# The seams between the stages of two chained transformer blocks, taken by token tile

## What is computed

```python
x = x + 0.5 * gate0 * swiglu(modulate(x, w0, shift0, scale0), w13[0], w2[0])     # FFN 0, 2816 hidden
x = x + gate1 * hybrid_mixer(modulate(x, w1, shift1, scale1), ...)               # attention and convolution
x = x + 0.5 * gate2 * swiglu(modulate(x, w2, shift2, scale2), w13[1], w2[1])     # FFN 1
h = rmsnorm(x, norm_mix_g)                                                       # second block
x = x + (gate_a * y_a(h) + gate_b * y_b(h)) @ w_out
x = x + square(relu(rmsnorm(x, norm_mlp_g) @ w_ff1)) @ w_ff2
x = x + sigmoid(rmsnorm(x, norm_ple_g) @ w_ple_gate) * (p @ w_ple)
return rmsnorm(x, final_norm_g)

def modulate(x, w, shift, scale): return rms_norm(x, w) * (1 + scale) + shift
def rmsnorm(x, g): return x * rsqrt(mean(x * x, -1) + 1e-6) * g
```

## Time and profile before

| | us |
|---|---|
| median of 3 runs | 1082.72 |
| lowest, highest | 1081.56, 1084.91 |
| the profiled execution: own time | 1081.31 |
| its span | 1079.4 |
| TensorE busy in the span | 1020.7 |
| VectorE (DVE) busy | 696.8 |
| ScalarE (ACT) busy | 501.0 |

### The profile page before, as it was taken

The page is one execution under the profiler, slowest core; times in us unless marked ns, Lnnn a source line. Parts: engine busy times, 40 slices in busy tenths (PEclk is TensorE's granted clock), DMA queues, the critical chain, the costliest instruction groups (busy, mean ns, idle before and its releaser), DMA issues.

```text
span 1079.4 us, 12967 instructions
## 1 busy us (share of the span) xinstructions
PE 1020.7 (95%) x4788; PEld 839.2 (78%) x4788; DVE 696.8 (65%) x1040; ACT 501.0 (46%) x554; POOL 36.7 (3%) x70
## 2 busy tenths in 40 slices
PE   7999999899989889999999999899999999999996
PEld 5877888688777767888888787777787778888874
DVE  6968777878868667654445895354556565445557
ACT  5553334444664435433344555543453444444452
POOL 0001111001001000000000000000000000000000
PEclk9999999989999999999999999998999999999999
DMA  9967998647637335875455545233334455544531
GB/s 382 414 235 273 329 307 314 236 163 277 269 126 264 117 117 183 317 270 182 186 194 194 224 176 195 78 117 116 128 117 156 179 208 189 195 174 176 195 117 39
DMA packets 37038, 219.41 MB, mean 203 GB/s; under 512 B 4192, under 2 KB 4960, under 8 KB 16006
## 3 DMA queue, kind: packets, MB, share of 16 engines
q1 hardware_dynamic: 26604, 179.70, 44.9%
q0 software_dynamic: 9104, 35.66, 9.4%
q10 hardware_dynamic: 1290, 3.51, 0.9%
HBM read 217.77 MB, written 4.22 MB: 206 GB/s over the span
## 4 chain that ended last, share of the span: by engine, by line
PE 77%; DVE 13%; ACT 5%; DMA 2%; issue 1%; ACTq 0%; DVEq 0%; POOLq 0%; SPq 0%
PE YP L402 11%; PE YP L404 11%; PE YP L403 11%; PE GP L402 10%; PE GP L404 10%; PE GP L403 10%; DVE wlo L1494 4%; ACT whi L1015 2%; PE TP L404 2%; PE TP L403 2%; PE TP L402 2%; DVE arena L1635 1%; DMA raw<-in_stream 1%; DMA ada<-in_ada_t 1%; DVE ada L1626 1%
## 5 line engine op out<-in xcount | busy, mean ns | idle before, releaser
L1494 DVE TENSOR_TENSOR wlo<-raw,whi 128x2048 fp32r<-128x2048 f32 x160 | 365.5, 2290 | 198.2 <-ACT whi L1015 197.9
L1015 ACT ACTIVATE whi<-raw 128x2048 fp32r<-128x2048 f32 x160 | 306.0, 1918 | 281.0 <-PE YP L404 144.4
L402 PE MATMUL GP<-whi,hT 128*128 128x512 f32 x512 | 203.0, 396 | 6.2 <-DVE hT L1584 2.3
L404 PE MATMUL GP<-whi,hT 128*128 128x512 f32 x512 | 199.9, 390 | 0.0
L403 PE MATMUL GP<-wlo,hT 128*128 128x512 f32 x512 | 199.6, 390 | 0.0
L402 PE MATMUL YP<-whi,hT 128*128 128x512 f32 (+2 forms) x320 | 130.2, 407 | 7.0 <-DVE hT L1575 2.5
L402 PE MATMUL YP<-whi,bT 128*128 128x512 f32 x334 | 131.4, 393 | 0.3 <-DVE bT L1681 0.3
L404 PE MATMUL YP<-whi,bT 128*128 128x512 f32 x334 | 130.2, 390 | 0.0
L403 PE MATMUL YP<-wlo,bT 128*128 128x512 f32 x334 | 130.0, 389 | 0.0
L403 PE MATMUL YP<-wlo,hT 128*128 128x512 f32 (+2 forms) x320 | 124.5, 389 | 0.0
L404 PE MATMUL YP<-whi,hT 128*128 128x512 f32 (+2 forms) x320 | 124.3, 389 | 0.0
(11 more groups left out here) (314 smaller groups left out, 1031.8 us busy)
## 6 DMA issues: line engine op xcount, KB each, us to landing
raw<-in_stream SPq DMA_DIRECT2D x161, 1024.0 KB, 4.8
ada<-in_ada_t POOLq DMA_DIRECT2D x48, 512.0 KB, 5.4
arena<-in_ada_t SPq DMA_DIRECT2D x8, 1024.0 KB, 10.7
arena<-in_ada_t POOLq DMA_DIRECT2D x8, 512.0 KB, 6.1
bias_scratch<-bias_row POOLq DMA_DIRECT2D x1, 3072.0 KB, 15.2
ada<-bias_scratch POOLq DMA_DIRECT2D x8, 384.0 KB, 3.9
arena<-in_b_gate ACTq DMA_DIRECT2D x2, 1024.0 KB, 6.5
x<-in_x SPq DMA_DIRECT2D x2, 512.0 KB, 4.0
```

Of the source, the lines that this page charges most:

```text
L402: nc.tensor.matmul(out_ap, xT[0][:, k, tok], hi, start=start, stop=False)
L404: return nc.tensor.matmul(out_ap, xT[1][:, k, tok], hi, start=False, stop=stop)
L1015: nc.scalar.activation(whi[:, slot, :], raw[:, slot, :], ACT.Copy).then_inc(w_hi, 1)
L1494: nc.vector.tensor_tensor(wlo[:, slot, :], raw[:, slot, :], whi[:, slot, :].bitcast(F32), ALU.subtract)\
```

## The change

All five seams go by token tile. The fourth quarter of the residual no longer stands before tile 0's squares and factor. Squares are taken in halves of 512 columns with the factor 1/32 squared in them; the factor has eight operations instead of nine and comes out scaled by RS_SCALE (undone in modA, in the gain row, and by a ninth operation in seams 3 to 5). In seams 1 and 2 ACT scales the left half of a tile and DVE the right half (in seam 2, tile 0, DVE both). The eight transposes of one tile (`turn_tile`) are one step; ACT's shift goes over 128 columns and is followed, for chunks 2 to 7 of tile 0 and all of tile 1, by ACT's own rounding; DVE subtracts. TensorE takes tile 0 through all eight chunks of the two units, and then tile 1 (`project_first`); tile 1's transposes are put in before its first chunk in seams 1 and 2, and before chunk 6 or 4 of tile 0 in seam 3 or 4 and 5. Tile 0's transposes move into the stage before: in seams 3 and 5 ahead of its last quarter of rows, in seam 2 ahead of the last two chunks, in seam 4 ahead of the last four. The bias rows move out of FFN 0 into seam 1. The hand-written orders of ACT and DVE mix the pieces of the residual, of both tiles and of the units' `hi` and `lo`. Not shown below are merged semaphores (`dve_step` for several others, `b_gate`, `bias_in`, `last_loaded`), renamed tiles, and the removed helpers.

```diff
+        ACT_HI = (range(2, KD), range(KD))
...
+            def turn_tile(phase, t):
+                for k in range(KD):
+                    if k % 4 == 0:
+                        if phase < 3:
+                            pe.wait_ge(sig(f"x_{('left', 'right')[k // 4]}{t}"), phase + (t == k // 4))
+                        else:
+                            pe.wait_ge(sig(f"x_part{t}"), summed(phase, k // 4))
+                    if t and k % 2 == 0:
+                        pe.wait_ge(sig("h0"), ready(phase, 0, k + 1))
+                    last = nc.tensor.transpose(x_bank(phase, k)[:, tok(t)],
+                                               (xn if phase < 3 else x)[:, t, k * P:(k + 1) * P], ident[:, :])
+                    if k % 2:
+                        last.then_inc(sig(f"turned{t}"), 1)
+            def project_first(phase, u, outs, insert, width=N):
 
                 for t in range(T):
-                    if phase < 3:
-                        pe.wait_ge(sig(f"x_scaled{t}"), phase + 1)
-                    else:
-                        pe.wait_ge(sig("x_summed"), T * (phase - 1) + t + 1)
                     for k in range(KD):
-                        last = nc.tensor.transpose(x_bank(phase, k)[:, t * P:(t + 1) * P],
-                                                   (xn if phase < 3 else x)[:, t, k * P:(k + 1) * P], ident[:, :])
-                        if t == T - 1 and k % 2:
-                            last.then_inc(sig("x_turned"), 1)
+                        if (t, k) == insert:
+                            turn_tile(phase, 1)
+                        if t == 0 and k % 4 == 0:
+                            pe.wait_ge(w_lo, u + k // 4 + 1)
+                        pe.wait_ge(sig(f"h{t}"), ready(phase, t, k))
+                        last = passes(outs[t][:, 0:width], (hT_hi, hT_lo), k, t, (u + k // 4) % SLOTS, k % 4 * N, width,
+                                      k == 0, k == KD - 1)
+                        if t == T - 1 and k % 4 == 3:
+                            last.then_inc(w_used, 1)
...
-            def last_rows(units, xT):
+            def last_rows(units, xT, phase=None):
 
                 for v in units:
                     pe.wait_ge(w_lo, v + 1)
                 for t, n in by_tile:
+                    if (t, n) == by_tile[-1] and phase is not None:
+                        turn_tile(phase, 0)
                     for m, v in enumerate(units):
                         for j in range(2):
                             last = passes(bank(YP, 2 * t + n), xT, 2 * m + j, t, v % SLOTS, (2 * j + n) * N, N,
                                           False, v == units[-1] and j == 1)
-                    if (t, n) == by_tile[-1]:
-                        last.then_inc(w_used, len(units))
-                        return
-                    last.then_inc(sig("y_part"), 1)
-            def project_tiles(u, xT, nk, outs, each=None):
+                        if (t, n) == by_tile[-1]:
+                            last.then_inc(w_used, 1)
+                    if (t, n) != by_tile[-1]:
+                        last.then_inc(sig("y_part"), 1)
+            def project_tiles(u, xT, nk, outs, phase=None, at=None):
...
+                        if t == T - 1 and k == at:
+                            turn_tile(phase, 0)
...
+            pe.wait_ge(sig("gate_row"), 2)
+            bias_row(0, bank(GP, 0))
+            pe.wait_ge(sig("x_part0"), summed(1, 1))
+            bias_row(1, bank(YP, 1))
+            pe.wait_ge(sig("x_part1"), summed(1, 0))
+            bias_row(2, bank(YP, 2))
+            pe.wait_ge(sig("bvec_set"), 1)
+            turn_tile(1, 0)
+            project_first(1, U_C0, Y01, (1, 0), C0)
...
-            project_tiles(U_WO + 2, x_hl, KD, T01)
-            turn_x(2)
+            project_tiles(U_WO + 2, x_hl, KD, T01, 2, 6)
             swiglu(1, U_FFN[1])
-            turn_x(3)
-            project(U_KVA, x_hl, KD, Y01, N, ("hT", KD * 3))
+            project_first(3, U_KVA, Y01, (0, 6))
...
+            project_first(4, U_FF, [bank(GP, 0), bank(GP, 1)], (0, 4))
...
-            last_rows([U_PLE + 1, U_PLE + 2], hidT)
             pe.wait_ge(sig("ple_copied"), 4)
-            turn_x(5)
-            project(U_PGATE, x_hl, KD, [bank(YP, 0), bank(YP, 1)], N, ("hT", KD * 5))
+            last_rows([U_PLE + 1, U_PLE + 2], hidT, 5)
+            project_first(5, U_PGATE, [bank(YP, 0), bank(YP, 1)], (0, 4))
...
+            def square(phase, t, n):
+                act.wait_ge(sig(f"x_part{t}"), summed(phase, n))
+                nc.scalar.activation(xn[:, t, part(n)], x[:, t, part(n)], ACT.Square, scale=1.0 / 32,
+                                     accum_out=xs[:, 2 * n, t:t + 1]).then_inc(sig(f"squares{t}"), 1)
+            def left(phase, t):
+                act.wait_ge(sig("x_rs"), T * phase + t + 1)
+                nc.scalar.activation(xn[:, t, part(0)], x[:, t, part(0)], ACT.Identity, scale=xs[:, 3, t:t + 1])\
...
+            def shifted(phase, t, ks):
+                act.wait_ge(sig("mod_ready"), phase)
+                for k in ks:
+                    act.wait_ge(sig(f"turned{t}"), turned(phase, t, k))
+                    nc.scalar.activation(hy[:, k, tok(t)], x_bank(phase, k)[:, tok(t)], ACT.Identity,
+                                         bias=mod[:, 24 * phase + k:24 * phase + k + 1], scale=modA[:, k:k + 1])\
+                        .then_inc(sig(f"hy_ready{t}"), 1)
+                    if k in ACT_HI[t]:
+                        act.wait_ge(sig(f"hy_ready{t}"), ready(phase, t, k))
+                        nc.scalar.activation(hT_hi[:, k, tok(t)], hy[:, k, tok(t)], ACT.Copy)\
+                            .then_inc(sig(f"h_hi{t}"), 1)
+            def gained(phase, t, gain, ks=range(KD)):
+                for k in ks:
+                    act.wait_ge(sig(f"turned{t}"), turned(phase, t, k))
+                    nc.scalar.activation(hT_hi[:, k, tok(t)], x_bank(phase, k)[:, tok(t)], ACT.Identity,
+                                         scale=col(gain, k)).then_inc(sig(f"h_hi{t}"), 1)
...
-            squares(1)
-            scale_first(1)
+            square(1, 0, 0)
+            square(1, 0, 1)
+            square(1, 1, 0)
+            bias_copy(0, bank(GP, 0))
+            left(1, 0)
+            shifted(1, 0, range(4))
+            square(1, 1, 1)
+            shifted(1, 0, range(4, KD))
+            left(1, 1)
+            bias_copy(1, bank(YP, 1))
+            bias_copy(2, bank(YP, 2))
+            shifted(1, 1, range(KD))
+            act.wait_ge(sig("bvec_set"), NG)
+            act.dma_start(bias_row[:, :], bvec[0:HB, :]).then_inc(sig("bias_row_stored"), 16)
             his(U_C0 + 2, U_C0 + 3)
-            shift_scale(1, 24)
             act.dma_start(causal[:, :], A["causal"]).then_inc(sig("causal_loaded"), 16)
...
-            squares(2)
-            scale_first(2)
-            shift_scale(2, 48)
-            his(60, 62)
+            for t in range(T):
+                square(2, t, 0)
+            square(2, 0, 1)
+            his(60, 61)
+            shifted(2, 0, range(4))
+            square(2, 1, 1)
+            shifted(2, 0, range(4, KD))
+            left(2, 1)
+            shifted(2, 1, range(KD))
+            his(61, 62)
             swiglu(1, U_FFN[1])
-            squares(3, [0])
-            norm_hi(3, "mix")
-            squares(3, [1])
+            gained(3, 0, "mix")
+            gained(3, 1, "mix")
+            for t, n in by_tile:
+                square(3, t, n)
             his(U_KVA + 2, U_KVA + 3)
...
-            squares(4, [0])
-            norm_hi(4, "mlp")
-            squares(4, [1])
+            gained(4, 0, "mlp")
             his(U_FF + 1, U_FF + 2)
+            gained(4, 1, "mlp")
+            for t, n in by_tile:
+                square(4, t, n)
             his(U_FF + 2, U_FF + 3)
...
-            squares(5, [0])
-            norm_hi(5, "ple")
-            squares(5, [1])
-            his(158, UNITS)
+            gained(5, 0, "ple")
+            his(158, 159)
+            gained(5, 1, "ple")
+            for t, n in by_tile:
+                square(5, t, n)
+            his(159, UNITS)
...
-                    squares(6, [t])
+                    square(6, t, 0)
+                    square(6, t, 1)
...
+            def split(phase, t, ks):
+                for k in ks:
+                    hi_, lo_ = hT_hi[:, k, tok(t)], hT_lo[:, k, tok(t)]
+                    if k in ACT_HI[t]:
+                        dve.wait_ge(sig(f"h_hi{t}"), hi_count(phase, t, k))
+                    else:
+                        dve.wait_ge(sig(f"hy_ready{t}"), ready(phase, t, k))
+                        link(nc.vector.tensor_copy(hi_, hy[:, k, tok(t)]))
+                    nc.vector.tensor_tensor(lo_, hy[:, k, tok(t)], hi_.bitcast(F32), ALU.subtract)\
+                        .then_inc(sig(f"h{t}"), 1)
...
-            residual(1, U_FFN[0] + 33, ybank, 0)
-            norm_x(1)
+            residual(1, 0, 0, U_FFN[0] + 33, ybank, 0)
```

(76 more changed lines are left out.)

252 lines of the change are left out of this document (102 added, 150 removed).

## The result

| kernel | median, us | lowest, highest | ratio to before, 95% interval |
|---|---|---|---|
| before, 20 runs | 1081.18 | 1078.17, 1088.84 | |
| changed, 20 runs | 1092.33 | 1083.79, 1097.5 | 1.0093 [1.0072, 1.0114] |

The change makes the kernel slower by 0.9%, some 10 us; 1094 was predicted, in 1078 to 1105. The medians lie 11.2 us apart, the profiled executions 9.8 (1091.13 and 1081.31, with spans of 1089.3 and 1079.4).

A forecast was written before the change was run, and what follows sets the result against it. TensorE, busy for 95% of the span, was taken as the bound. Seam terms sum to +5.1 us and lost clock adds 7.1, about +12 on 1081.3, or 1093.3; adjusted to the median, about 1094, range 1078 to 1105.

The forecast's parts named there:

- rival A: The forecast itself: ACT's queue puts the next unit's split behind tile 1, clock falls after the gaps; 1094 us, chance 0.50.
- The prices: ACT's 128-column shift plus rounding (a pair) costs 0.72 us, between 0.48 and 0.98; DVE's 128-column operation 0.28.
- Rival C: The seams shrink because ACT's pair costs near its floor of 0.48, without a clock fall; 1078 us, chance 0.15.
- Seam 1: After FFN 0: units 35 and on start at 234.3 instead of 231.5, +2.8 us, with TensorE idle 3.9 us.
- Seam 2: After the mixer: first silu moves from 420.40 to about 422.6, +2.2 us; TensorE idles 5.9 us.
- Seam 3: Ahead of the second attention's projections: late rest parts and rounding cost +2.2 us, plus 1 for units that follow.
- Seams 4 and 5: Last two seams: waits for chunks and the next unit's rest part mostly go, -1.7 and, with the tail, -1.4 us.
- The clock: Half clock behind the new gaps in seams 2, 1 and 3 costs 7.1 us; no fall seen after waits of 0.8 and 1.6.
- the old falls: Earlier clock falls in seams 1 and 2: their cost isn't regained, since TensorE waits for ACT there anyway.
- Other edits: Merged semaphores, extra scalings, units' slots and the bias rows' three matmuls: costed at nothing, under 1 us if uncovered.

The follow-up runs named there:

- e1: Changed kernel with unit 35's rounding moved ahead of scaling tile 1's left half, and its rest part ahead of tile 1's subtractions, in seam 1: 1088.63 us, ratio 1.0061.
- e2: Changed kernel with unit 61's rounding and rest part ahead of tile 1's work in seam 2, unit 62's behind the first silu and product: 1085.00 us, ratio 1.0029.
- e3: Changed kernel with unit 93's rest part ahead of tile 0's chunks and unit 94's split ahead of tile 1's, in seam 3: 1084.30 us, ratio 1.0029.
- e6: Changed kernel with unused transposes of the identity filling TensorE's waits in seams 1, 2 and 3: 1087.60 us, ratio 1.0057.
- e5: Kernel before, with ACT's rounding of units 125 and 158 ahead of tile 1's squares in seams 4 and 5: 1077.68 us, ratio 0.9980.
- e4: Changed kernel with the next units' splits moved in seams 1, 2 and 3, and unit 34's rest part behind chunks 2 and 3: 1072.00 us, ratio 0.9905.

## Why the prediction was right

**The bound and the mechanism.** The forecast, rival A, named one step as the cause: the next unit's `hi` and rest part behind tile 1's work, in seams 1, 2 and 3. e1, e2 and e3 took it away one seam at a time, and 7.2, 4.5 and 7.7 us went with it, in single executions, between which a seam of the changed kernel that was left alone varied by up to 0.7; together the three took 20 us from the median. That is shown.

**The prices.** A pair on ACT was taken as 0.72. It is 0.69 (from 228.93 to 229.62 in the timeline): shift 0.44, rounding 0.31. Half the columns bring the shift from 0.49 per chunk to 0.44 alone. Rival C needed 0.48 for a pair, and is out by that row. The 0.28 that the forecast gives for DVE's subtraction of 128 columns was the row of another operation (L1594, a scaling of the identity); the changed kernel's subtraction takes 0.29, so nothing hangs on it.

**Seam 1.** Unit 35 was to start at 234.3 and did, but seen from FFN 0's end, which came 1.7 earlier, the wait is +4.5 and not +2.8. What I missed: the gap of 2.7 ahead of chunk 2 already brought the clock down (0.72 in the window 214 to 226), so tile 1's transposes came late, and ACT, which I took for busy all the time, waited 2.6 us for them. With 1.7 of clock behind the gap the seam is +6.0 against +5.2. In e2 and e3 less clock was lost in the first gap and more in the second, and the seam costs the same.

**Seam 2.** Forecast: silu +2.2, idle 5.9, and 3.4 of clock, 5.6 in all. Measured: 2.8 (430.20 against 420.40 and the 7.0 from before the seam), 5.6, and 1.7; 4.9 in all. The fall was half as dear as the one I took it from, which was luck of this execution: behind the same wait the clock was 0.72 over 12 us in e1 and e3, 3.4 lost, just the price taken, and the seam cost 5.2 and 5.3 there.

**Seam 3.** +3.2 and 1.4 of clock forecast, 6.1 measured, with waits of 3.0, 1.4 and, at a later projection, 1.9 (I had allowed 1 for what follows).

**Seams 4 and 5.** -1.7 and, with the tail, -1.4 forecast; -1.9 and -2.3 measured. In seam 4 neither chunk nor `wlo` is waited for. In seam 5 a `wlo` wait of 0.5 stays.

**The clock.** 7.1 forecast, 5.1 by the windows, 3.9 to 4.7 by e6's time. My reading that waits of up to 1.6 are safe was wrong, and the trace of the kernel before would have told: I looked at the seams alone, but its clock is 0.57 in 317 to 321, at a wait of 1.6, and 0.54 in 726 to 737, behind one of 1.0. The forecast also took the old falls as free; e5's profile, with 3.4 us less of lost clock in seam 1, is 2.3 shorter there. A wait of 1.6 in the mixer's attention, in both kernels, was followed by the high clock before and by the low one after the change. The same stage in two windows, the kernel before and then the changed one:

```profile
360.00:364.00 4.00, 3.86 (x17) 3.24 (x18) 2.49 (x6) 3.86 (x3) 0.00 (x0) 1.00 0.02 6
```

```profile
364.00:368.00 4.00, 3.65 (x9) 2.90 (x10) 2.49 (x6) 3.99 (x3) 0.00 (x0) 0.50 0.01 2
```

That is the +2.8 in the mixer; the -4.0 in the second attention is the old kernel's fall there, which the changed one's profile lacks and e1's, e3's, e4's and e6's have. As the falls there come and go between executions, I take these two for chance; they nearly cancel, and belong to no step of the change.

**Other edits, at nothing.** This term was wrong, in the good direction. The bias rows' matmuls stood in FFN 0, where TensorE had passes to do at once. The kernel before, TensorE:

```profile
76.41 1.02 PE L544 MATMUL TP<-arena 33*4 33x512 f32 x2
...
83.03 1.02 PE L544 MATMUL TP<-arena 33*4 33x512 f32 x2
```

Each costs TensorE 1.1 to 1.2 us with its surroundings, and all nine kernels with the rows' new place gain 1.1 and 1.2 at these two points of the count (0.6 is lost again some 60 passes later). In the seam they lie beside ACT and DVE, partly in the gap.

So the mechanism was right, and that the sum came so near was in part luck, since errors cancelled: seams 1 and 3 dearer by 0.8 and 1.5, seams 2, 4, 5 and the bias rows cheaper by 0.7, 0.2, 0.9 and 1.7 to 2.3. The forecast +12 stands against +9.8 in the profiles and +11.2 in the medians, and its 1094 starts from a median of 1082.7 that 20 runs put at 1081.2.

## What to carry to other kernels

When a step is cut into smaller ones, look at what stands behind it in the in-order queues, and first at the next stage's operand preparation: here the kernel with tile-wise seams lost 0.9% with it behind and gained 0.95% with it in the engines' idle times. Put such long, independent instructions where the trace shows their engine waiting for a result that will come anyway. Compare two traces by the time at which equal numbers of the bounding engine's instructions have begun; it separates what came from untouched stages from what the change did. Take more than one execution of each, as the clock alone moved a stage by up to 3.9 us here.
